# All input and modulation requests issued at the start, modulation weights as the moving operand, and norm stages in 384- and 128-token tails with interleaved squares and roundings

## The reference

```python
shift, scale, gate = jnp.split(jax.nn.silu(c) @ w_mod[l] + b_mod[l], 3, axis=-1)
shift_c, scale_c, gate_c = jnp.split(jax.nn.silu(c_ctx) @ w_mod[l] + b_mod[l], 3, axis=-1)
h = rms_norm(x, norm_w[l]) * (1.0 + scale[:, None, :]) + shift[:, None, :]
hc = rms_norm(xc, norm_w[l]) * (1.0 + scale_c) + shift_c
parts = split_in(h @ w_in[l])
...
# the second block, same form with its own weights
h = rms_norm_2(x, norm_mix[l]) * (1.0 + scale_m) + shift_m
```

## Time and profile before

| | |
|---|---|
| median of 3 runs | 4618.35 us (4615.28 to 4619.43) |
| profiled execution, its own time | 4615.54 us |
| its span in the trace | 4613.7 us |
| mean granted TensorE clock | 0.915 of full speed |
| PE busy | 3988.9 us (86%) |
| DVE, ACT, POOL busy | 2089.2, 1548.8, 652.5 us |
| start of the first norm stage's factors | 141.48 us from the start of the span |
| first matmul after the first norm stage | 194.26 us |

### The profile page before, as it was taken

The page is one execution under the profiler, slowest core; times in us unless marked ns, Lnnn a source line. Parts: engine busy times, 40 slices in busy tenths (PEclk is TensorE's granted clock), DMA queues, the critical chain, the costliest instruction groups (busy, mean ns, idle before and its releaser), DMA issues. The chain is left out here.

```text
span 4613.7 us, 42989 instructions
## 1 busy us (share of the span) xinstructions
PE 3988.9 (86%) x16492; PEld 2886.4 (63%) x16492; DVE 2089.2 (45%) x2604; ACT 1548.8 (34%) x2420; POOL 652.5 (14%) x332
## 2 busy tenths in 40 slices
...
DMA packets 354838, 451.03 MB, mean 98 GB/s; under 512 B 51981, under 2 KB 227266, under 8 KB 354130
## 3 DMA queue, kind: packets, MB, share of 16 engines
...
## 5 line engine op out<-in xcount | busy, mean ns | idle before, releaser
L1189 PE MATMUL values<-probs,vp 128*128 128x512 f32 x672 | 348.4, 600 | 12.0 <-issue 6.4
L1277 ACT ACTIVATE probs<-scores 128x512 f32<-128x512 f32 (+1 forms) x336 | 196.0, 583 | 306.3 <-PE scores L213 304.6
L211 PE MATMUL scores<-q_hi,k_rest 97*128 97x512 f32 (+1 forms) x336 | 262.2, 780 | 0.0
L3417 PE MATMUL dp<-h_t,abt 128*128 128x512 f32 x544 | 241.9, 597 | 1.1 <-ACT abt L3466 0.9
L3448 ACT ACTIVATE expert_hi<-wu 128x1024 fp32r<-128x1024 f32 x136 | 144.7, 1064 | 250.4 <-PE gp L213 250.4
L255 POOL TENSOR_TENSOR ring_r<-ring_w,ring_hi 128x1024 fp32r<-128x1024 f32 x44 | 116.7, 2654 | 758.7 <-ACT ring_hi L248 758.7
L1358 DVE TENSOR_REDUCE mx<-made 128x1 f32<-128x640 f32 (+1 forms) x272 | 203.7, 793 | 27.3 <-PE made L1130 26.5
L211 PE MATMUL smb<-x_t_r,merge_w_r 128*128 128x512 f32 x480 | 196.0, 408 | 19.1 <-POOL merge_w_r L2758 16.4
L211 PE MATMUL gates_ps<-x_t_r,ring_r 128*128 128x512 f32 (+1 forms) x560 | 206.2, 368 | 2.9 <-PEq L81 2.9
L779 DVE SCALAR_TENSOR_TENSOR conv_out<-conv_in,vectors,conv_out 128x1295 f32<-128x1295 f32 (+1 forms) x120 | 205.5, 1713 | 4.3
L212 PE MATMUL gates_ps<-h_t_r,ring_hi 128*128 128x512 f32 (+1 forms) x560 | 206.2, 368 | 0.0
...
## 6 DMA issues: line engine op xcount, KB each, us to landing
...
```

The lines of the kernel that those rows point to most:

```text
L211: nc.tensor.matmul(out, lhs[1], rhs[0], start=start, stop=False, **kw)
L1189: nc.tensor.matmul(O[b % 2][:, 0:w], vp[g // 2 % 2][:, kb, g % 2 * VD:g % 2 * VD + P], pr[m % 3][:, 0:w], start=kb == 0, stop=kb == nk - 1 ...
L1277: nc.scalar.activation(pr[m % 3][:, 0:w], S[m % 2][:, 0:w], ACT.Exp, scale=scale).then_inc(s.exped, 1)
L3417: m = nc.tensor.matmul(dp[half][:, :], at[:, j, :], wd[u][:, j, half * 512:(half + 1) * 512], start=j == 0, stop=j == FK - 1)
```

## The change

It has three parts. `opening` joins `load_vectors` and `turn_in`, drops `modulation`, `gemm` and the separate Silu stage, and gives each of ten input tiles and eight weight pieces a buffer and a semaphore of its own (the tiles lie in the memory of `k.h`). ACT issues these 18 requests (ten of 512 KB with rows of 4 KB, eight of 1.5 MB with rows of 12 KB) at the start, while SP issues the vectors' requests; only after its 18 does ACT wait for the turned vectors. The turned tiles have two PSUM buffers where there were four, since the modulation's sums take the other six banks.

The modulation is computed the other way round: the two condition columns are the stationary operand and 512 columns of weights the moving one, 48 matmuls into two rows of 3072 numbers in PSUM. ACT and DVE copy half of the rows each, PE turns them in 24 small transposes, and DVE adds the bias.

In the norm stages with `kept`, the last block of 512 tokens is split into 384 and 128, ACT alternates one square of block i with one rounding of block i-1, the ring roundings stand ahead of the last block's squares, DVE takes the rests of a block straight after its multiplications, and SP issues the ring loads after the stores of two blocks.

```diff
--- before.py
+++ after.py
@@ -41,6 +41,8 @@
 CTX_BLOCK = (0, CTX, 1)
 X_BLOCKS = [(CTX, 512, 0), (CTX + 512, 512, 0)]
 ALL_BLOCKS = [CTX_BLOCK] + X_BLOCKS
+X_NORMS = [(CTX, 512, 0), (CTX + 512, 384, 0), (CTX + 896, 128, 0)]
+ALL_NORMS = [CTX_BLOCK] + X_NORMS
 
 
 def named(**values):
@@ -144,7 +146,7 @@
     return rows, tiles
 
 
-def load_vectors(nc, k, a):
+def load_vectors(nc, k, a, o):
 
     rows, tiles = vector_rows(a)
     k.at = {name: (tile, row) for name, tile, row, _, _, _, _ in rows}
@@ -164,6 +166,15 @@
             sp.wait_ge(s.cleared, 2)
             for _, tile, row, n, ap, first, width in rows:
                 sp.dma_start(raw[row:row + n, tile, first:first + width], ap).then_inc(s.rows_in, 16)
+
+        @block.scalar
+        def _(act):
+            for i, (ap, _) in enumerate(o.tiles):
+                act.dma_start(o.rows[:, i, :], ap).then_inc(o.tile_in[i], 16)
+            for j in range(DK):
+                act.dma_start(o.w[:, j, :], a.w_mod[0][j * P:(j + 1) * P, :]).then_inc(o.w_in[j], 16)
+            act.wait_ge(s.turned, 1)
+            nc.scalar.activation(k.vec[:, :, :], ps[:, :, :], ACT.Copy).then_inc(s.copied, 1)
 
         @block.tensor
         def _(pe):
@@ -173,11 +184,6 @@
             for t in range(4):
                 last = nc.tensor.transpose(ps[:, t, :], raw[:, t, :], k.ident)
             last.then_inc(s.turned, 1)
-
-        @block.scalar
-        def _(act):
-            act.wait_ge(s.turned, 1)
-            nc.scalar.activation(k.vec[:, :, :], ps[:, :, :], ACT.Copy).then_inc(s.copied, 1)
 
 
 def col(k, name, i=0, n=1, rows=P):
@@ -404,65 +410,6 @@
             extra[1](block, s, walk, lambda eng, sem, value: eng.sem_inc(sem, value))
 
 
-def gemm(nc, k, name, parts, rhs, widths, dk=DK, extra=None, slots=2):
...
 def cols_of(w, first, pair):
 
     return w.rearrange("(k p) n -> p k n", p=P)[:, :, bass.ds(pair * 256 + first, 256)]
@@ -476,20 +423,6 @@
         def _(act):
             for i, name in enumerate(names):
                 nc.scalar.activation(dst[:, :, i], col(k, name, 0, DK), ACT.Silu).then_inc(s.done, 1)
-
-
-def modulation(nc, k, name, w, bias, n_chunks, dst, conds):
-
-    silu_columns(nc, k, k.cond, conds)
-    tile, row = k.at[bias]
-
-    def evac(p, c, b, ps, slot):
-        at = 2 * p + (row + c)
-        return nc.scalar.activation(dst[:, bass.ds(2 * p + c, 1), :], ps, ACT.Identity,
-                                    bias=k.vec[:, tile, bass.ds(at, 1)])
-
-    gemm(nc, k, name, [(n_chunks // 2, lambda p: cols_of(w, 0, p), evac)],
-         lambda j, b: k.cond[:, j, :], [2], slots=4)
 
 
 AHEAD = D
@@ -512,7 +445,7 @@
 
 
     src, dst = k.x, k.h
-    names = "kept0 kept1 kept2 cleared squared summed logged root_ready scaled shifted rounded rest"
+    names = "kept0 kept1 kept2 kept3 cleared squared summed logged root_ready scaled shifted rounded rest"
     with ExitStack() as es, stage(nc, names) as s, nc.Block() as block:
         sq = [es.enter_context(sbuf(nc, f"rm_sq{i}", [P, 512], F32)) for i in range(4)]
         lg = es.enter_context(sbuf(nc, "rm_log", [P, 512], F32))
@@ -522,10 +455,10 @@
         if kept is not None:
             @block.sync
             def _(sp):
-                if ring:
-                    for n in range(2):
-                        load_half(sp, ring, n, columns)
                 for i, (t0, w, _) in enumerate(blocks):
+                    if ring and i == 2:
+                        for n in range(2):
+                            load_half(sp, ring, n, columns)
                     sp.dma_start(kept[:, :, t0:t0 + w], src[:, :, t0:t0 + w]).then_inc(s.all[i], 16)
                 for i in range(len(blocks)):
                     sp.wait_ge(s.all[i], 16)
@@ -534,16 +467,16 @@
         def _(act):
             nc.scalar.preload_act_table_set(LN_EXP)
 
-            def round_block(act, i):
+            def round_chunk(i, j):
                 t0, w, which = blocks[i]
-                act.wait_ge(s.all[i], 16)
-                for j in range(DK):
-                    act.wait_ge(s.scaled, i * DK + j + 1)
-                    nc.scalar.activation(k.x_r[:, j, t0:t0 + w], dst[:, j, t0:t0 + w], ACT.Identity,
-                                         bias=mod[:, shift_at + j, which:which + 1]).then_inc(s.rounded, 1)
+                if j == 0:
+                    act.wait_ge(s.all[i], 16)
+                act.wait_ge(s.scaled, i * DK + j + 1)
+                nc.scalar.activation(k.x_r[:, j, t0:t0 + w], dst[:, j, t0:t0 + w], ACT.Identity,
+                                     bias=mod[:, shift_at + j, which:which + 1]).then_inc(s.rounded, 1)
 
             for i, (t0, w, _) in enumerate(blocks):
-                if ring and i == 1:
+                if ring and i == len(blocks) - 1:
                     for n in range(2):
                         round_half(nc, ring, act, n)
                 for j in range(DK):
@@ -552,6 +485,8 @@
                         act.wait_ge(s.summed, n - 3)
                     nc.scalar.activation(sq[n % 4][:, 0:w], src[:, j, t0:t0 + w], ACT.Square)\
                         .then_inc(s.squared, 1)
+                    if kept is not None and i:
+                        round_chunk(i - 1, j)
                 act.wait_ge(s.summed, (i + 1) * DK)
                 nc.scalar.activation(lg[:, 0:w], ps[i % 2][:, 0:w], ACT.Ln, bias=k.eps, scale=1.0 / D)\
                     .then_inc(s.logged, 1)
@@ -560,10 +495,9 @@
                     act.wait_ge(s.scaled, (i - 1) * DK)
                 nc.scalar.activation(root[i % 2][:, 0:w], lg[:, 0:w], ACT.Exp, scale=-0.5)\
                     .then_inc(s.root_ready, 1)
-                if kept is not None and i:
-                    round_block(act, i - 1)
             if kept is not None:
-                round_block(act, len(blocks) - 1)
+                for j in range(DK):
+                    round_chunk(len(blocks) - 1, j)
 
         @block.tensor
         def _(pe):
@@ -593,10 +527,8 @@
                     nc.vector.scalar_tensor_tensor(dst[:, j, t0:t0 + w], src[:, j, t0:t0 + w],
                                                    factor[:, j, which:which + 1], root[i % 2][:, 0:w],
                                                    ALU.mult, ALU.mult).then_inc(s.scaled, 1)
-                if kept is not None and i:
-                    take_rest(i - 1)
-            if kept is not None:
-                take_rest(len(blocks) - 1)
+                if kept is not None:
+                    take_rest(i)
 
         if ring:
             @block.gpsimd
@@ -620,42 +552,65 @@
 
 
 
-def turn_in(nc, k, dst, sources):
-
-    tiles = [(ap[i * P:(i + 1) * P, :], t0 + i * P) for ap, t0 in sources for i in range(ap.shape[0] // P)]
-    with ExitStack() as es, stage(nc, "in0 in1 turned copied") as s, nc.Block() as block:
-        raw = [es.enter_context(sbuf(nc, f"ti_raw{i}", [P, D], F32)) for i in range(2)]
-        ps = [es.enter_context(psum(nc, f"ti_ps{i}", [P, 4, P], F32)) for i in range(4)]
-        row_in = (s.in0, s.in1)
-
-        @block.sync
-        def _(sp):
-            for i, (ap, _) in enumerate(tiles):
-                if i >= 2:
-                    sp.wait_ge(s.turned, 2 * (i - 1))
-                sp.dma_start(raw[i % 2][:, :], ap).then_inc(row_in[i % 2], 16)
+def turn_in(nc, k, dst, o, conds):
+
+    with ExitStack() as es, stage(nc, "turned copied silu_done rows_made rows_kept cols_made biased") as s, nc.Block() as block:
+        n_chunks = 3 * DK
+        mod_rows = es.enter_context(sbuf(nc, "mod_rows", [2, n_chunks * P], F32))
+        rows_ps = es.enter_context(psum(nc, "mod_rows_ps", [2, n_chunks * P], F32))
+        ps = [es.enter_context(psum(nc, f"ti_ps{i}", [P, 4, P], F32)) for i in range(2)]
+        cols_ps = ps[0][:, 0, 0:2 * n_chunks].rearrange("p (n i) -> p n i", i=2)
+        halves = 2 * len(o.tiles)
+        per_bank = 512
 
         @block.tensor
         def _(pe):
-            for i in range(len(tiles)):
-                pe.wait_ge(row_in[i % 2], 16 * (i // 2 + 1))
-                for h in range(2):
-                    n = 2 * i + h
-                    if n >= 4:
-                        pe.wait_ge(s.copied, n - 3)
-                    for q in range(4):
-                        c = 4 * h + q
-                        last = nc.tensor.transpose(ps[n % 4][:, q, :], raw[i % 2][:, c * P:(c + 1) * P], k.ident)
-                    last.then_inc(s.turned, 1)
+            for n in range(halves):
+                i, h = divmod(n, 2)
+                if h == 0:
+                    pe.wait_ge(o.tile_in[i], 16)
+                if n >= 2:
+                    pe.wait_ge(s.copied, n - 1)
+                for q in range(4):
+                    c = 4 * h + q
+                    last = nc.tensor.transpose(ps[n % 2][:, q, :], o.rows[:, i, c * P:(c + 1) * P], k.ident)
+                last.then_inc(s.turned, 1)
+            pe.wait_ge(s.silu_done, 2)
+            for j in range(DK):
+                pe.wait_ge(o.w_in[j], 16)
```

(56 more changed lines are left out.)

43 lines of the change are left out of this document (removed).

## The result

The changed kernel takes 4587.0 us, median of four runs (4582.0 to 4590.2), and the kernel before 4618.9 beside it (4615.3 to 4622.7): a ratio of 0.993, 95% interval 0.9913 to 0.9947. The profiled execution took 4586.5, its span is 4584.7. The forecast was 4581, with a range of 4545 to 4602.

What follows compares the result with a forecast made beforehand. Most stages were taken as bound by TensorE, the modulation by PE at 1.2 GHz. Opening 23.2 plus norm stages 14 gave 37.2 off 4615.5, 4578.3, or 4581 us against the median; range 4545 to 4602.

Steps and rivals of the forecast that it cites:

- V: Opening: moment at which all 45 vector requests are in; taken as 50 us, near the bulk's earliest end, against 17.8 before.
- rival (a): Opening: the vector requests are not held by the bulk and are in at about 20 us; 4551 us; chance 0.25.
- Issues on ACT: Opening: ACT's 18 issues can hold it until part of the bulk drains; hidden behind late vectors, otherwise up to some 10 us.
- The opening's sum: Opening: vectors 50, next start 2.3, tiles 16, modulation 48.8, exit 1.2; factors at 118.3 instead of 141.5, saving 23.2 us.
- Tiles 16: Opening: turning the ten input tiles takes 16 us, within bounds 12 and 17.3, once all tiles are there.
- Modulation 41: Opening's modulation: 48 products of 512 columns, 96 records, take 41 us on PE at 2.4 GHz.
- rival (c): Modulation's clock stays at 1.2 GHz and the vectors wait until 57 us; 4628, slower by 10; chance 0.07 for both together.
- Copies 1.8: Opening's modulation: ACT and DVE each copy out half of the rows, 1536 columns each, in at most 1.8 us.
- The small transposes: Opening's modulation: 24 small transposes on PE take at most 5.2 us, taken as an upper end from large ones at 0.216 each.
- Factors at 118.3: End of the opening: modulation factors ready at 118.3 us instead of 141.5.
- The norm stages: Norm stages: 5.2 us saved in each of two layers, 3.8 in the second block; together 14.2, taken as 14.
- The end: Whole kernel: 23.2 + 14 = 37.2 us off 4615.5, a stage's saving passing to the end one for one.

## Why the prediction was right, and where it was not

**The vectors (V 50).** Measured 53.2, near the end of the bulk, which flowed at 392 to 431 GB/s to 45 us, at 325 to 50 and at 15 after that. What was wrong is the row that I read for rival (a): a gather of 512 KB beside a busy queue says nothing of 45 small requests. The reason that I gave for 50, that they follow each other on few engines, was argued from a busy share; the packets between 40 and 50 us (25 of SP's beside 22 of ACT's for each engine) speak for it, but no trace names the engines. What the runs do show is that smaller pieces on the other queue free them (28.6). By the Trainium skill ("DMA: Bandwidth & Descriptors", Queues, rings and completion order) an engine alternates between queues packet by packet, and V is then near the end of the bulk. The trace agrees: 53.2 with pieces of 12 KB, 28.6 with pieces of 1.5 KB.

**Issues on ACT.** I had up to 10 us, hidden. Measured: from 1.5 to 17.4 us, 15.9 in all, hidden behind V. Where V is early it shows: 13.8 us of idle PE in the run with the vectors first.

**The opening's sum.** Tiles 16, measured 15.1. Modulation 41 for 96 records, measured 41.36 at a granted clock of 0.98; rival (c) fell. Copies 1.8, measured 1.75. The small transposes were the term most off, 5.2 for 2.2: I took the upper end, each like a transpose of 128 columns. Factors at 118.3, measured 117.4: 24.1 gained for 23.2; V was 3.2 too early, and the other terms together 4.1 too long.

**The norm stages.** From factors to the next stage's first product: layer 0 52.8 to 48.3, 4.4 gained for 5.2; layer 1 54.9 to 48.6, 6.3 for 5.2; second block 50.1 to 46.9, 3.2 for 3.8. Sum 13.9 for 14.2. That this is so near is partly luck. These are differences of single profiles, and in the second profile of the kernel before layer 0's stage took 55.1, which would make its gain 6.8. The mechanism came true in one case of four. I foresaw that DVE's multiplications of 384 columns would wait for POOL, as those of 256 had in the earlier trace rows, and that the stage would end on DVE. In layer 0 of the second profile that is so (8.51 us, end at 164.33). In layer 0 of the first and in layer 1 of both it was POOL that waited, and the stage ended on it; at 48.2 to 48.6 us the length is the same either way. The failed step is to carry the collision over as if it were the instructions' own: in the earlier trace rows DVE had resumed 1.0 us before POOL came, after 8.56 us of idle time; now it had mostly run for 11.3 us without a pause. The rule of the Trainium skill ("SBUF — State Buffer", SBUF: two separate sides) is that whoever starts first holds the shared ports for a whole instruction, and the other blocks. The traces agree where one instruction of DVE is held for one of POOL's (2.44 to 2.71 us instead of 0.48 or 0.62). Why DVE's next instruction gets the ports first, again and again, in a run without a pause, isn't shown by any run here.

**The end.** 37.2 forecast; 38.0 can be read directly in the touched stages (24.1 and 13.9), and with what shifted in the stages between them the gain was 42.8 at the second block's first product. Between the two profiled executions it is 29.1. The step that failed is that a saving in a stage passes to the end one for one. In the profiles about 12 us went in the second block, in stages whose code is the same, above; why, stays open. By the terms alone the median would be 4580 (4615.5 less 38, and 2.8 more); it is 4587, still inside the range.
